# Expert weights of the fixed places loaded during the output projections, one persistent weight ring, and a new order of places in layer 2

## The reference, cut to what matters

```python
for layer in range(DEPTH):
    ...                                   # mixer; its output times w_out, gated, added to h
    t = modulate(rmsnorm(h, norm2_w[layer]), sh2, sc2)
    g = top1(softmax(t @ w_group)); e = top2 of the 4 experts in group g
    f = sum over the two: gate * (silu(t @ w_gate[g, e]) * (t @ w_up[g, e])) @ w_down[g, e]
    h = h + g2 * f
return rmsnorm(h, final_norm_w)
```

## Time and the profile before

| | |
|---|---|
| median of three runs | 1779.41 us |
| profiled execution | 1780.7 us, of which 1778.8 us is the span from first to last instruction |
| mean granted TensorE clock | 0.929 of full speed |
| PE busy | 1506.4 us (85%), 7011 instructions |
| DVE / ACT / POOL busy | 806.2 / 466.8 / 240.7 us |
| DMA | 353.92 MB, mean 199 GB/s |
| queue q1 (issued by SP) / q0 (by POOL) / q10 (by ACT) | 277.78 / 61.79 / 13.18 MB |

### The profile page before, as it was taken

One profiled execution on the slowest core, in us unless ns is written; L12 is line 12 of the kernel. 1 busy time (PEld: TensorE's weight loads), 2 busy tenths in 40 slices (PEclk: granted clock), 3 DMA queues, 4 the chain that ended last, 5 costly groups with the idle time before them and its releaser, 6 DMA issues. The chain is left out here.

```text
span 1778.8 us, 18329 instructions
## 1 busy us (share of the span) xinstructions
PE 1506.4 (85%) x7011; PEld 787.7 (44%) x7011; DVE 806.2 (45%) x1317; ACT 466.8 (26%) x957; POOL 240.7 (14%) x246
## 2 busy tenths in 40 slices
PE   4999998999997999799991999649969999649942
PEld 2566554444445777445540333224435554413310
DVE  2136655888842667354324111126546763422214
ACT  5122112000106677221110111023226651100002
POOL 0000000000002685322001000021000001010001
PEclk9999998999998999999995999869979999869976
DMA  8444435777783998733119799662040003399964
GB/s 324 142 130 148 148 107 172 270 281 283 278 246 94 304 279 257 281 114 140 36 52 376 273 356 339 261 254 104 12 90 7 1 1 119 137 383 353 394 259 153
DMA packets 164423, 353.92 MB, mean 199 GB/s; under 512 B 17217, under 2 KB 106641, under 8 KB 145521
## 3 DMA queue, kind: packets, MB, share of 16 engines
q1 hardware_dynamic: 143496, 277.78, 45.2%
q0 software_dynamic: 17056, 61.79, 9.1%
q10 hardware_dynamic: 3785, 13.18, 1.9%
HBM read 296.67 MB, written 56.05 MB: 198 GB/s over the span
## 5 line engine op out<-in xcount | busy, mean ns | idle before, releaser
L595 PE MATMUL ie_pu<-aT_even,ie_w_conv 128*128 128x512 f32 (+1 forms) x640 | 207.4, 486 | 0.0
L2129 PE MATMUL ex_ps_gu<-room,ex_xT 128*32 128x512 f32 x1472 | 170.4, 615 | 31.2 <-DMA room<-in_moe_w_up_dram 27.8
L595 PEld LDWEIGHTS ie_pu<-aT_even,ie_w_conv 128*128 128x128 f32 x640 | 121.2, 190 | 84.6 <-issue 76.5
L1647 PE MATMUL po_ps_y<-po_w,po_yT 128*128 128x512 f32 x320 | 139.1, 592 | 2.0 <-DVE po_n L1546 2.0
L641 PE MATMUL ie_pu<-yacc_even,aT_even 128*128 128x512 f32 x288 | 127.4, 603 | 8.4 <-ACTq L745 8.4
L641 PE MATMUL ie_pu<-hacc,aT_even 128*128 128x512 f32 x288 | 125.2, 593 | 0.0
L2129 PEld LDWEIGHTS ex_ps_gu<-room,ex_xT 128*32 128x32 f32 x1472 | 57.3, 114 | 138.8 <-issue 134.3
L2246 DVE TENSOR_TENSOR ex_hid<-ex_hid,ex_ps_gu 128x256 f32<-128x256 f32 x25 | 10.5, 421 | 215.4 <-ACT ex_hid L2200 215.4
L769 DVE SCALAR_TENSOR_TENSOR yacc_even<-ie_pu,pcol,yacc_even 128x255 f32<-128x255 f32 x80 | 47.5, 614 | 107.7 <-ACT yacc_even L722 106.2
L1647 PEld LDWEIGHTS po_ps_y<-po_w,po_yT 128*128 128x128 f32 x320 | 60.0, 190 | 74.0 <-issue 71.7
L641 PEld LDWEIGHTS ie_pu<-yacc_even,aT_even 128*128 128x128 f32 x288 | 55.3, 193 | 78.8 <-issue 78.8
(11 more groups left out here) (466 smaller groups left out, 2308.3 us busy)
## 6 DMA issues: line engine op xcount, KB each, us to landing
room<-in_moe_w_gate_dram SPq DMA_DIRECT2D x33, 1024.0 KB, 11.5
room<-in_moe_w_up_dram SPq DMA_DIRECT2D x33, 1024.0 KB, 13.9
room<-in_moe_w_down_dram SPq DMA_DIRECT2D x33, 1024.0 KB, 8.9
ie_w_conv<-in_ada_w_dram SPq DMA_DIRECT2D x27, 1024.0 KB, 5.3
yacc_even<-in_ada_w_dram SPq DMA_DIRECT2D x13, 1024.0 KB, 5.4
y<-ex_y ACTq DMA_DIRECT2D x25, 512.0 KB, 8.1
room<-ac_rows SPq DMA_DIRECT2D x12, 1024.0 KB, 6.8
ie_w_conv<-in_ev_w_in_dram SPq DMA_DIRECT2D x10, 1024.0 KB, 6.0
```

Source lines behind the costliest of these rows:

```text
L595: last = nc.tensor.matmul(pu[t][:, a:b], w_conv[h][:, k, t * P:(t + 1) * P], aT[:, k, a:b], start=(k == 0), stop=(k == KD - 1))
L1647: last = nc.tensor.matmul(ps_y[:, c * BANK:(c + 1) * BANK], yT[n % 2][:, k, :] if even else kit.oT[:, k, n * P:(n + 1) * P], (w[:, k] if e ...
L2129: last = MM(ps_gu[s][rows, :, :], xT[s][:, k, rows], wgu[q % RING][:, :, k, :], start=(k == 0), stop=(k == KD - 1))
```

## The change

Layer 1's working tiles (`yacc`, `hacc`, `room`, the weights `w` of the output projection) are now views of the weight ring `room5`, which exists for the whole program. Tile n of `yacc` and `hacc` together is exactly as large as one weight piece. In the output projection of layer 1, SP loads a weight piece of places 0 and 1 into the room of tile n once that tile's `t` rows are stored: five of the six pieces; the sixth is loaded in routing. In the output projection of layer 2, SP issues all nine pieces of now three fixed places, three after each of `load_h(1)`, `load_h(2)` and `load_h(3)`; they go to slots 0, 1 and 4, which attention has left. In routing `plan` is worked out right after the rank, so `named` comes earlier, and the small rows for the next stage are loaded later, by the expert stage's SP after the fifth place of its loop (`fgate` and `fw` stay in routing). In layer 2 the strips are `[4,4,4,0,4,4,3,3,3,2,2,2,2,1,1,1]` instead of `[4,4,0,4,4,3,3,3,3,2,2,2,2,2,1,1]`, place 3 instead of place 2 is the empty one, and the ring is filled in the order of slots 0, 1, 4, 2, 3.

```diff
-        under = [tile[:, :, :].rearrange("p t d -> p (t d)") for tile in (kit.yacc, kit.hacc)]
+        under = [kit.rows[:, a * (NT + 1) * D:(a + 1) * (NT + 1) * D] for a in range(2)]
...
-    kit.room = scope.enter_context(kit.nc.sbuf_tensor("room", [P, 20 * TOK], F32))
+    after = kit.room5[:, 2 * (NT + 1) * D:RING * SLOT]
+    kit.room, kit.beside = after[:, 0:20 * TOK], after[:, 20 * TOK:20 * TOK + 2 * BANK]
...
-        w = sb("w", [P, K, D]) if even else None
+        w = kit.room5[:, 2 * (NT + 1) * D:RING * SLOT].rearrange("p (k d) -> p k d", d=D) if even else None
...
-        h_stored, t_stored = [S(f"h_stored{j}") for j in range(2)], S("t_stored")
+        h_stored, t_stored = ([S(f"{n}{j}") for j in range(2)] for n in ("h_stored", "t_stored"))
...
+            def early_rows(n):
+                sp.wait_ge(t_stored[n % 2], n // 2 * 16 + 16)
+                load_early(kit, sp, layer, n)
 
             if even:
                 for q in range(K // PIECE):
@@ -1388,6 +1395,13 @@
                 if n + 1 < count:
                     load_in(n + 1)
                 load_h(n)
+                if not even:
+                    for piece in range(3 * (n - 1), 3 * n):
+                        load_early(kit, sp, layer, piece)
+                elif n >= 2:
+                    early_rows(n - 2)
+            if even:
+                early_rows(count - 2)
 
...
-                pool.dma_start(kit.t[rows_T, :], yrow(n)).then_inc(t_stored, 16)
+                if n >= 2:
+                    pool.wait_ge(t_stored[n % 2], n // 2 * 16)
+                pool.dma_start(kit.t[rows_T, :], yrow(n)).then_inc(t_stored[n % 2], 16)
...
+        self.first = {q: self.items.index(q) // LANES for q in order}
+        self.last = {q: (len(self.items) - 1 - self.items[::-1].index(q)) // LANES for q in order}
+        self.base = [LANE * self.items.index(q) if strips[q] else 0 for q in range(NEXP)]
+        self.slot = {q: ring[i % RING] for i, q in enumerate(order)}
+        self.nth = {q: i // RING + 1 for i, q in enumerate(order)}
+        self.before = {q: order[i - RING] if i >= RING else None for i, q in enumerate(order)}
+        self.whole = ring[len(order) % RING]
+        self.times = [len([q for q in order if self.slot[q] == s]) for s in range(RING)]
+        self.ends = [max(self.last[q] for q in order if self.slot[q] == s) for s in range(RING)]
...
-PLACES = [Places(NT, 2, [5, 5, 2, 5, 5, 4, 4, 4, 3, 3, 3, 2, 2, 2, 2, 1]), Places(NT - CT, 2, [4, 4, 0, 4, 4, 3, 3, 3, 3, 2, 2, 2, 2, 2, 1, 1])]
+PLACES = [Places(NT, 2, [5, 5, 2, 5, 5, 4, 4, 4, 3, 3, 3, 2, 2, 2, 2, 1], list(range(NEXP)), [0, 1, 2, 3, 4]),
+          Places(NT - CT, 3, [4, 4, 4, 0, 4, 4, 3, 3, 3, 2, 2, 2, 2, 1, 1, 1], [0, 1, 2, 4, 5, 6, 7, 8, 9, 10, 11, 12, 13, 14, 15], [0, 1, 4, 2, 3])]
+EARLY = [2 * 3 - 1, 3 * 3]
...
-            for q in range(places.fixed):
-                kit.load_gu(sp, q, q)
-                kit.load_d(sp, q, q)
-            sp.wait_ge(kit.t_stored, 16 * N)
-            if layer == 0:
-                kit.load_odd_small(sp)
-            else:
-                kit.load_final(sp)
+            for tiles_stored in kit.t_stored:
+                sp.wait_ge(tiles_stored, 16 * (N // 2))
+            for piece in range(EARLY[layer], 3 * places.fixed):
+                load_early(kit, sp, layer, piece)
+            if layer:
+                kit.load_final_row(sp)
             sp.wait_ge(named, 1)
-            for q in range(places.fixed, RING):
-                if places.strips[q]:
+            for q in places.order[:RING]:
+                if q >= places.fixed:
                     e = sp.value_load(kit.plan[0:1, q:q + 1], min_val=0, max_val=NEXP - 1)
-                    kit.load_gu(sp, e, q)
-                    kit.load_d(sp, e, q)
+                    kit.load_gu(sp, e, places.slot[q])
+                    kit.load_d(sp, e, places.slot[q])
...
+            ch(TT(by_place[:, :, :], across(place[:, :]), down(tab[:, R_NUM:R_NUM + NEXP]), ALU.is_equal))
+            ch(TT(by_place[:, :, :], by_place[:, :, :], across(tab[:, R_NUM:R_NUM + NEXP]), ALU.mult))
+            ch(RED(ident[:, :], by_place[:, :, :], AX.X, ALU.add))
+            ch(V.tensor_copy(kit.plan[:, 0:NEXP], ident[:, :]))
+            dve.sem_inc(named, 1)
             ch(TT(at_place[:, :, :], down(place[:, :]), across(tab[:, R_NUM:R_NUM + NEXP]), ALU.is_equal))
...
-            ch(TT(by_place[:, :, :], at_place[:, :, :].rearrange("p e r -> p r e"), across(tab[:, R_NUM:R_NUM + NEXP]), ALU.mult))
-            ch(RED(ident[:, :], by_place[:, :, :], AX.X, ALU.add))
-            V.tensor_copy(kit.plan[:, 0:NEXP], ident[:, :]).then_inc(named, 1)
...
+    def load_c(sp, e, s, c):
+        sp.dma_start(kit.wgu[s][:, c, :, :], kit.w_views[c][bass.ds(e, 1)].rearrange("a p k f -> p (a k) f")).then_inc(kit.wgu_loaded[s], 16)
...
+def load_early(kit, sp, layer, piece):
+    q, c = piece // 3, piece % 3
+    if c < 2:
+        kit.load_c(sp, q, PLACES[layer].slot[q], c)
+    else:
+        kit.load_d(sp, q, PLACES[layer].slot[q])
...
-            for q in range(RING, NEXP):
+            for i, q in enumerate(places.order[RING:]):
                 e = sp.value_load(kit.plan[0:1, q:q + 1], min_val=0, max_val=NEXP - 1)
-                o = before(q)
-                if o is not None:
-                    sp.wait_ge(gu_ready, places.last[o] + 1)
-                kit.load_gu(sp, e, q % RING)
-                if o is not None:
-                    sp.wait_ge(d_ready, places.last[o] + 1)
-                kit.load_d(sp, e, q % RING)
-            sp.wait_ge(d_ready, places.last[before(NEXP)] + 1)
+                sp.wait_ge(gu_ready, places.last[places.before[q]] + 1)
+                kit.load_gu(sp, e, slot[q])
+                sp.wait_ge(d_ready, places.last[places.before[q]] + 1)
+                kit.load_d(sp, e, slot[q])
+                if i == 4:
+                    if layer == 0:
+                        kit.load_odd_small(sp)
+                    else:
+                        kit.load_final(sp)
+            sp.wait_ge(d_ready, places.ends[WHOLE] + 1)
...
-                        pe.wait_ge(wgu_loaded[q % RING], 32 * nth(q))
+                        pe.wait_ge(wgu_loaded[slot[q]], 32 * nth[q])
...
+    def load_rows(sp):
         sp.dma_start(kit.fx[:, :, :], kit.h_mid[CTX:TOK, :].rearrange("(t p) d -> p t d", p=P)).then_inc(kit.fx_loaded, 16)
 
...
+        kit.room5 = kit.keep("room5", [P, RING * SLOT])
+        kit.slot = [kit.room5[:, s * SLOT:(s + 1) * SLOT] for s in range(RING)]
...
-            kit.yacc, kit.hacc = hold(scope, "yacc_even", [P, NT + 1, D]), hold(scope, "hacc", [P, NT + 1, D])
+            kit.rows = kit.room5[:, 0:2 * (NT + 1) * D]
+            kit.yacc, kit.hacc = (kit.rows.rearrange("p (t a d) -> p t a d", a=2, d=D)[:, :, a, :] for a in range(2))
```

More of the change, by code:

```diff
@@ L352, in phase_in_even @@
         tokens = [tok_all[:, h, :, :] for h in range(2)]
-        stage = [sb(f"stage{s}", [P, BANK]) for s in range(4)]
+        stage = [kit.beside[:, s * BANK:(s + 1) * BANK] for s in range(2)] + [sb(f"stage{s}", [P, BANK]) for s in range(2, 4)]
         r = {n: kit.room[0:NDT, j * TOK:(j + 1) * TOK] for j, n in enumerate(("x", "e", "ac", "f", "b", "ln", "dt", "da", "keepf", "keepb"))}
@@ L1306, in phase_out @@
     PIECE = 2
+    begin_weights(kit, layer)
     with ExitStack() as st:
@@ L1747, with __init__ @@
 class Places:
-    def __init__(self, tiles, fixed, strips):
-        self.fixed, self.strips = fixed, strips
-        self.items = [q for q, n in enumerate(strips) for _ in range(n)]
-        assert len(strips) == NEXP and len(self.items) % LANES == 0
+    def __init__(self, tiles, fixed, strips, order, ring):
+        self.fixed, self.strips, self.order = fixed, strips, order
+        self.items = [q for q in order for _ in range(strips[q])]
+        assert len(strips) == NEXP and len(self.items) % LANES == 0 and sorted(order) == [q for q in range(NEXP) if strips[q]]
         self.passes = len(self.items) // LANES
-        self.first = [self.items.index(q) // LANES if n else None for q, n in enumerate(strips)]
-        self.last = [(len(self.items) - 1 - self.items[::-1].index(q)) // LANES if n else None for q, n in enumerate(strips)]
-        self.base = [LANE * sum(strips[:q]) for q in range(NEXP)]
+        self.first = {q: self.items.index(q) // LANES for q in order}
[7 more added lines that the diff above has]
+        self.ends = [max(self.last[q] for q in order if self.slot[q] == s) for s in range(RING)]
         rows, price, most = tiles * P * 2, sorted(LANE * n + 1 for n in strips), 0
@@ L1853, in _ @@
             pool.wait_ge(slots_ready, 1)
-            pool.wait_ge(kit.t_stored, 16 * N)
+            for tiles_stored in kit.t_stored:
+                pool.wait_ge(tiles_stored, 16 * (N // 2))
             kit.gather_experts(pool)
@@ L1981, with begin_weights @@
 SLOT = 3 * KD * FF
-def begin_room(kit, scope, layer):
```

(26 more changed lines are left out.)

13 lines of the change are left out of this document (7 added, 6 removed).

## The result

The changed kernel takes 1792.79 us (median of 4 runs, 1790.95 to 1793.88), the kernel before 1779.76 beside it (4 runs, 1777.31 to 1781.45): ratio 1.0073, 95% interval 1.0061 to 1.0085. It is slower by 0.7%, 4.8 us later than the forecast of 1788 and inside the range. The profiled execution took 1793.88 with a span of 1792.0, 13.2 more than the span before.

What follows compares the result with a forecast made beforehand. PE, busy 85%, was taken to stand still for `gate_up`'s weights (27.8 us) and, at the experts' start, for the second gather. Terms 3.5 - 1.8 + 0.5 - 1.3 + 1.7 + 4.8 + 0.9 = +8.3 us gave 1788, range 1774 to 1798.

Steps and rivals of the forecast that it cites:

- Output projection of layer 2: Three early weight pieces compete with POOL's rows, so `vec` lands late and `turn_columns` waits: +3.5 us, bounds 0.4 and 4.6.
- rival 1: Layer 2's output projection: POOL's rows keep half the bandwidth, `vec` late by only 0.4 us; 1785 us, chance 0.14.
- `fx` in the ring: Layer 2's experts: 2.1 MB go in at the end of `down(4)`, `gate_up(8)` waits longer: +1.7 us, bounds 0 and 4.
- `gate_up(9)`: Layer 2's experts: new strips leave six pieces to issue after `down(7)`, lengthening this wait: +4.8 us, bounds 3.2 and 6.1.
- Place 15's down and the chunk: End of layer 2's experts: `down(9)` starts 3 us later, mostly covered by the chunk's wait: +0.9 us, bounds 0 and 2.
- Gathers: Routing: gathers meet fewer queued bytes and land sooner, gaining 1.8 us in layer 1 and 1.3 in layer 2.
- Small loads in the ring: Layer 1's experts: 2.8 MB enter after the fifth place, the late queue mostly recovers: +0.5 us, bound above +6.7.
- a sign that would refute me: Layer 1's experts: the forecast is wrong if pass 11 waits over 3 us.
- Layer 1's output projection: Five early pieces each delay row loads by some 2.5 us, hidden by PE's products: cost nothing.
- Rival 2: Gathers land as in quiet stretches, gaining 8 + 5 us instead of 3.1; about 1778 us, no change, chance 0.09.
- Rival 3: Layer 2's experts are bound by bytes, so the waits of 1.25 and 16.36 us vanish; about 1763 us, chance 0.10.
- Rival 4: Layer 1's ring: issuing small loads holds SP for 14 us, nothing is recovered: +6.2 us more, 1794 us, chance 0.11.

Runs made afterwards that it cites:

- e3: Changed kernel with layer 2's `fx` (the final stage's residual rows, 2 MB) loaded in routing again; 1787.61 us, ratio 1.0048.
- e2: Changed kernel with other strips, so that places 8, 9 and 10 end in passes 6, 7 and 7 as in the kernel before; 1786.07 us, ratio 1.0031.
- e4: Changed kernel with layer 1's eight small loads issued in routing again, before the weights; 1791.88 us, ratio 1.0073.
- e5: Changed kernel with no weights loaded in the output projections; all pieces of the fixed places issued at the start of routing; 1785.02 us, ratio 1.0037.
- e6: Changed kernel with layer 1's small loads back in routing and no weights loaded in either output projection; 1792.79 us, ratio 1.0071.
- c2: c1 with `plan` worked out after the placing, as in the kernel before; 1776.27 us, ratio 0.9986.
- b1: Kernel before with only layer 1's eight small loads moved from routing to after the ring's fifth place; 1772.83 us, ratio 0.9970.
- c1: Changed kernel, layer 2's early pieces from the third residual tile on, places 8, 9, 10 ending in passes 6, 7, 7, `fx` in routing; 1774.4 us, ratio 0.9974.
- c3: c1 with no weights loaded in the output projections; 1773.57 us, ratio 0.9974.
- c4: c1 with early weight loads in layer 2's output projection only, none in layer 1's; 1771.47 us, ratio 0.9954.

## Why the prediction came out as it did

The direction, the two places and the mechanism were right; the sizes of two terms were not, and one small term had the wrong sign. Term by term, predicted and measured:

*Output projection of layer 2: +3.5, measured +8.9*, above the bound of 4.6. This is the main miss, in two parts. First, `po_vec` landed 15.9 us after its issue, and PE stood 6.0 longer than before. The DMA view of the kernel after: that issue, then the queues in windows of 1480 to 1487 and of 1487 to 1491 (columns as in the earlier trace rows):

```profile
po_vec<-mod POOLq DMA_DIRECT2D x2, 4.0 KB, 15.9
...
q1 hardware_dynamic: 270, 2.02, 68.4%
q0 software_dynamic: 269, 0.97, 34.2%
...
DMA  7698989977815011199799999898991000000000
...
q0 software_dynamic: 352, 0.92, 58.7%
...
h_mid<-po_h POOLq DMA_DIRECT2D x1, 512.0 KB, 3.6
```

The kernel before from 1480 to 1487, same view (a digit of the DMA line is the busy share, in tenths, of a fortieth of the window):

```profile
DMA  9998999999999999989799999997732111000000
...
q0 software_dynamic: 615, 1.88, 73.1%
```

POOL's queue got a third of the bytes, 0.14 MB per us against SP's 0.29, as the step assumed from the earlier trace rows. The end was about right too. Before, the queue is nearly alone from 1480, and almost all of its 1.88 MB is through when the DMA line falls, at 1485.1: some 0.36 MB per us, not far from the 0.42 that I used. After, SP's pieces end near 1487 and the rows' bytes near 1488.1; 0.52 MB of the second window are already the first store of `h_mid`. This stage starts 4.4 us earlier in the profile after (1470.6 against 1475.0), so 1488.1 is 1492.5 on the clock of before, where the step said 1492.2.

What the step left out is the time from the last bytes to the landing: I let `vec` land when the bytes were in. Before, it lands at 1486.8, 1.7 us after the DMA line falls; after, PE resumes at 1490.54, 2.4 us after the rows' bytes are in. With that 1.7 the step would have said 1492.2 + 1.7 + 0.3 = 1494.2, which is 5.3 us past 1488.94, against the measured 6.0. The kernel before has this tail with no store near it, so the store need not be its cause; the cause stays open.

Of the turns themselves the first window says more than I read from it: 270 packets against 269, of 7.5 and 3.6 KB. By these counts the queues took turns packet by packet, and the queue with small packets got fewer bytes. The Trainium skill (DMA: Bandwidth & Descriptors, Queues, rings and completion order) has turns per packet, a packet there being a group of descriptors; I had taken that for an equal split of bytes, which it isn't. The equal counts agree with turns; whether the profile's packets are the page's is not shown. So rival 1 read the rule wrongly and fell.

Second, the clock. Windows of the kernel after (columns as in the earlier trace rows), then of the kernel before over the same products:

```profile
1490.50:1500.50 10.00, 9.96 (x17) 4.37 (x18) 6.08 (x10) 0.20 (x1) 0.56 (x1) 0.70 0.13 53
...
1683.00:1692.40 9.40, 9.27 (x65) 2.58 (x65) 0.00 (x0) 0.00 (x0) 0.00 (x0) 0.75 0.77 316
...
1738.00:1743.80 5.80, 5.75 (x33) 1.50 (x34) 0.00 (x0) 0.00 (x0) 0.00 (x0) 0.63 1.02 429
```

```profile
1489.00:1496.00 7.00, 7.00 (x18) 3.17 (x18) 6.33 (x12) 2.64 (x4) 0.56 (x1) 1.00 0.19 75
1677.50:1684.60 7.10, 7.04 (x65) 2.44 (x65) 0.10 (x1) 0.00 (x0) 0.00 (x0) 1.00 0.88 337
```

After a wait of 5.96 us the granted clock of the next 10 us is 0.70, a mix of both levels, and 7.1 us of products take 10.0: +2.9. The prediction counted a stall as long as its wait. 6.0 + 2.9 = 8.9, the whole of the stage. The Trainium skill (TensorE: Matmul & The Clock Gate, HAM oscillation) says that a wait for DMA makes the products behind it start on the slow clock; the trace agrees for this wait, and I had not priced it.

*`fx` in the ring: +1.7, measured +5.2*, above its bound of 4. D(7) came 115.9 after the start instead of 110.7: the wait is 3.05 longer (predicted 1.7) and the products behind it 2.25 longer, at clock 0.75. In e3 the experts are 5.2 shorter again.

*`gate_up(9)`: +4.8, measured +4.3*, a wait of 20.6. The six-piece burst of layer 1 was a good model; e2 removes it. *Place 15's down and the chunk: +0.9, measured +1.1*: `down(9)` waited 5.47 instead of 1.50, and its products took 2.1 longer. The chunk's wait took back only 2.5 (2.16 instead of 4.63); another 2.7 came from the chunk's products, 7.13 instead of 9.86, at clock 1.00 instead of 0.72. The sum was right, and with two clock terms that I had not counted that was partly luck.

*Gathers: -1.8 and -1.3, measured -2.7 and -1.9* (total to experts, with the early plan in them). The second gather was issued 0.6 later after the total in both layers, where I had said 0.3, and PE started 3.3 and 2.5 sooner after that issue. The sizes are fair, the reason was half wrong. I wrote that moving small loads and `fx` makes room; e3 and e4 undo these with no loss at the gathers. e5 shows that layer 1 doesn't need the early pieces either. In layer 1 either of the two is enough (e6). In layer 2 both the plan's early end (c2) and the early pieces (e5, 1.5) help, but by how much each made the 1.9 is not shown.

*Small loads in the ring: +0.5, measured -1.2* (layer 1's experts as a whole). I feared a stretched queue; the profile shows pass 11 waiting 4.28, which I had named as a sign that would refute me, yet pass 12 waits 7.2 less. The term's sign was wrong, and in the kernel without early loads the same move gains 3.6 there (214.1 to 210.5, b1 against before). *Layer 1's output projection: 0*, and the total in layer 1 came no later. But with the early pieces layer 1's experts take 212.9 instead of 210.7 (e5), and 212.7 instead of 210.4 (c1 and c3). So the -1.2 is a gain of over 3 from the small loads less a loss of 2.2, which no term of the prediction has. Of that loss 1.3 stands in the first `gate_up`: 9.87 us at a granted clock of 0.70 against 8.53 at 0.81 in e5. c2, with early pieces and a late plan, takes 210.9, so the pieces alone do not make it; its cause is open.

Measured less predicted: 5.4 + 3.5 - 0.5 + 0.2 - 0.9 - 0.6 - 1.7, and -0.6 for the other stretches, give +4.8: 8.3 becomes 13.1. The two misses of 8.9 together were half covered by misses of the other sign, so that the total came within 5 us of the forecast is partly luck.

Rival 2 fell (gains of 4.6, not 13). Rival 3 fell as priced, but its idea has a place: once the strips are right, waits 8 and 9 have a sum of 17.2 to 17.9 in e2, c1 and c4, however it is divided between them. That bytes set this sum is my reading; no run tested it. Rival 4 gave nearly the right time for a wrong reason: SP issued the eight small loads in 6.0 us, not 14. The next place's gate went out 6.2 us later than in e4 (93.0 against 86.7 after the experts' start), and one pass later SP was level again (109.5 against 109.3).

Not tried: moving `turn_columns` behind `product(1, 0)`, which should hide the wait for `vec` even with the pieces where they are.

## What to carry to other kernels

Before you fill a quiet DMA stretch, look for the smallest row that is waited for in it: 4 KB rows behind 2 MB of broadcast rows and 3 MB of weights cost 9 us, and putting the weights one tile later cost nothing. When PE starts with a gather and not with a weight, earlier weights win next to nothing (1.5 us in layer 2, nothing in layer 1); take bulk that nobody needs yet out of the window of the gathers instead (one moved call: 6.8 us by stages, 3.6 to 6.2 by medians). After a change of places or strips, list for each place the pass that frees its slot, since one pass later there cost 4 to 7 us.
